# Second mixer: input chunks 5 to 7 go by token blocks behind the levels of the decayed scores

## The reference

```
cq, ckv, krope, gq, gk, gv, gg, lr_f, lr_b = _split(x @ w_in, ODD_SPLITS)
...
mla = _merge(_blocked_attention(q, k, v, (MLA_NOPE + MLA_ROPE) ** -0.5))
def log_gate(lr, w2, bias):
    return _heads(jax.nn.log_sigmoid((lr @ w2 + bias).astype(F32)) / GLA_TAU, GLA_HEADS)
gq_h = _heads(gq, GLA_HEADS) * (GLA_K_DIM ** -0.5)
o = _bidirectional_scan(gq_h, _heads(gk, GLA_HEADS), _heads(gv, GLA_HEADS), log_gate(lr_f, ...), log_gate(lr_b, ...))
gla = _merge(_rms_norm(o, gla_norm)) * jax.nn.silu(gg)
return jnp.concatenate([mla, gla], axis=-1) @ w_out
```

## Time and profile before

| | us |
|---|---|
| median of 3 runs | 2326.71 |
| lowest and highest | 2320.91, 2326.8 |
| span of the profiled execution | 2323.1 |
| TensorE busy in it | 2166.1 |
| VectorE busy | 1142.2 |
| ScalarE busy | 784.0 |

### The profile page before, as it was taken

How to read it: one execution, slowest core, us unless ns; L and a number is a source line. 1 busy time by engine, 2 the same in 40 slices (tenths; PEclk the granted TensorE clock), 3 DMA queues, 4 the chain that set the end, 5 groups by cost and what they waited for, 6 DMA issues and landing times.

```text
span 2323.1 us, 30109 instructions
## 1 busy us (share of the span) xinstructions
PE 2166.1 (93%) x12126; PEld 1528.0 (66%) x12126; DVE 1142.2 (49%) x1786; ACT 784.0 (34%) x1299; POOL 61.5 (3%) x62
## 2 busy tenths in 40 slices
PE   8999998899887989997988999999999999989998
PEld 7884443443367944433433688898888788888887
DVE  5582222121156831211111666678666766787666
ACT  3441110111034321101111355454555455554553
POOL 0010000000010100000000000001000000001000
PEclk9999999899998799999999999999999999999999
DMA  9449999999972289999999864634555464534561
GB/s 289 145 175 379 421 421 421 417 421 420 413 246 73 76 363 420 420 421 415 420 420 421 295 209 168 199 128 127 181 200 200 154 208 166 193 96 159 167 208 46
DMA packets 231542, 622.66 MB, mean 268 GB/s; under 512 B 15456, under 2 KB 166944, under 8 KB 182112
## 3 DMA queue, kind: packets, MB, share of 16 engines
q1 hardware_dynamic: 226096, 605.32, 68.7%
q0 software_dynamic: 3040, 10.78, 1.5%
q10 hardware_dynamic: 2256, 4.50, 0.5%
HBM read 619.51 MB, written 1.05 MB: 267 GB/s over the span
## 4 chain that ended last, share of the span: by engine, by line
PE 41%; DMA 6%; DVE 4%; ACT 2%; issue 1%; POOL 0%; SPq 0%; DVEq 0%; ACTq 0%
PE bank L1517 14%; PE bank L1505 10%; PE bank L1518 7%; PE bank L228 6%; PE bank L1345 3%; DMA arena<-in_moe_w_up 1%; DMA ring<-in_moe_w_up 1%; DMA ring<-in_ffn_gate 1%; DMA w_parts<-in_moe_w_up 1%; DMA x_tok<-in_moe_w_up 1%; DVE w_low L439 1%; PE bank L1673 1%; ACT w_high L432 1%; DVE x_tok L687 0%; DVE x_tok L676 0%
## 5 line engine op out<-in xcount | busy, mean ns | idle before, releaser
L439 DVE TENSOR_TENSOR w_low<-ring,w_high 128x1024 fp32r<-128x1024 f32 x364 | 441.1, 1225 | 271.7 <-ACT w_high L432 271.7
L1517 PE MATMUL bank<-xT_parts,w_high 128*128 128x512 f32 x1408 | 496.2, 395 | 6.0 <-DVE xT_parts L504 6.0
L432 ACT ACTIVATE w_high<-ring 128x1024 fp32r<-128x1024 f32 x364 | 377.1, 1053 | 218.0 <-PE bank L1518 184.6
L1518 PE MATMUL bank<-xT_parts,w_low 128*128 128x256 f32 x1408 | 394.5, 280 | 0.0
L1345 PE MATMUL bank<-ring,arena 128*64 128x512 f32 x1344 | 339.0, 594 | 17.3 <-DMA w_parts<-in_moe_w_gate 5.3
L1517 PEld LDWEIGHTS bank<-xT_parts,w_high 128*128 128x128 f32 x1408 | 264.0, 188 | 69.0 <-DVE xT_parts L504 6.9
L1345 PE MATMUL bank<-w_parts,arena 128*64 128x512 f32 x768 | 263.8, 609 | 13.4 <-DMA w_parts<-in_moe_w_up 6.7
L1518 PEld LDWEIGHTS bank<-xT_parts,w_low 128*128 128x128 f32 x1408 | 265.8, 189 | 3.1
L1345 PEld LDWEIGHTS bank<-ring,arena 128*64 128x64 f32 x1344 | 110.1, 137 | 230.5 <-issue 221.9
L1453 DVE SCALAR_TENSOR_TENSOR arena<-arena,bank 128x512 f32<-128x512 f32 x32 | 23.9, 747 | 434.1 <-PE bank L1345 434.1
L228 PE MATMUL bank<-w_high,xT_parts 128*128 128x256 f32 x1152 | 222.9, 290 | 10.4 <-DVE w_low L439 8.8
(11 more groups left out here) (284 smaller groups left out, 2934.4 us busy)
## 6 DMA issues: line engine op xcount, KB each, us to landing
ring<-in_moe_w_gate SPq DMA_DIRECT2D x56, 1024.0 KB, 24.3
ring<-in_moe_w_up SPq DMA_DIRECT2D x56, 1024.0 KB, 21.0
ring<-in_moe_w_down SPq DMA_DIRECT2D x56, 1024.0 KB, 25.8
ring<-in_ffn_gate SPq DMA_DIRECT2D x44, 1024.0 KB, 6.8
ring<-in_ffn_up SPq DMA_DIRECT2D x44, 1024.0 KB, 5.4
ring<-in_ffn_down SPq DMA_DIRECT2D x44, 1024.0 KB, 6.6
w_parts<-in_moe_w_up SPq DMA_DIRECT2D x32, 1024.0 KB, 26.1
w_parts<-in_moe_w_down SPq DMA_DIRECT2D x32, 1024.0 KB, 26.1
```

Source lines behind the costliest of these rows:

```text
L432: e.activation(hi, src, ACT.Copy).then_inc(*S.high.tell(key))
L439: e.tensor_tensor(lo, src, hi.bitcast(F32), ALU.subtract).then_inc(*S.low.tell(key))
L1517: e.matmul(pairs(bank[:, :]), hi[:, j, :], k.x_parts[:, :, j, :], start=j == 0, stop=False)
L1518: ins = e.matmul(bank[:, 0:T], lo[:, j, :], k.xh[:, j, :], start=False, stop=j == KT - 1)
```

## The change

Chunks 5, 6 and 7 leave the attention. The list loses its "project" entries. A table `OD_ROUNDS` says which token block of which chunk TensorE does behind which step of the levels: both blocks of 5 behind the diagonal and level 8, of 6 behind levels 7 and 6, of 7 behind levels 5 and 4. ScalarE copies each chunk out after its second block, and `OD_SPLITS` puts the split of chunk 7 behind that of level 8, and the split of output chunk 0 behind level 6; VectorE takes its part of those splits one step later. The split of chunk 6 moves ahead of the attention, behind the copy of chunk 4.

```diff
--- before.py
+++ after.py
@@ -1901,9 +1901,11 @@
 
 
 
-OD_ORDER = (("scores", 0), ("scores", 2), ("project", 5), ("gates", 0), ("probs", 0), ("probs", 2), ("project", 6), ("logs", 0),
+OD_ORDER = (("scores", 0), ("scores", 2), ("gates", 0), ("probs", 0), ("probs", 2), ("logs", 0),
             ("turn", 0), ("turn", 2), ("gates", 1), ("values", 0), ("values", 2), ("logs", 1),
             ("scores", 1), ("scores", 3), ("probs", 1), ("probs", 3), ("turn", 1), ("turn", 3), ("values", 1), ("values", 3), ("mix", 0), ("mix", 1))
+OD_ROUNDS = {0: (5, 0), 2: (5, 1), 3: (6, 0), 4: (6, 1), 5: (7, 0), 6: (7, 1)}
+OD_SPLITS = {2: ("od_in", 0, 7), 4: ("od_out", 0, 0)}
 ROPES = slice(MLA_NOPE, MLA_QD)
 
 
@@ -2004,9 +2006,7 @@
     project_pe(e, k, od(4))
     out_banks = [k.banks.open(e, O_BANKS, ("mla_o", pair)) for pair in range(2)]
     for what, i in OD_ORDER:
-        if what == "project":
-            project_pe(e, k, od(i))
-        elif what == "scores":
+        if what == "scores":
             view = pairs(k.banks.open(e, B_BANKS, ("mla", i))[:, :])
             e.wait_ge(*S.dve_step["q_roped", i // 2])
             e.wait_ge(*S.act_out["k_raw", 1])
@@ -2025,8 +2025,14 @@
             for j in range(2):
                 ins = mm(e, view[:, j, :], [(k.gla_w2[rank, block(j)], b.narrow_T[rank, 0, :])])
             ins.then_inc(*S.product.tell(("gate_log", i)))
-    project_pe(e, k, od(7))
-    decayed_pe(e, k, b.streams, lambda step: None)
+
+    def beside(step):
+        if step in OD_ROUNDS:
+            c, tb = OD_ROUNDS[step]
+            bank = k.banks.open(e, A_BANKS, od(c)) if tb == 0 else k.banks[od(c)]
+            project_block_pe(e, k, od(c), bank, tb)
+
+    decayed_pe(e, k, b.streams, beside)
     decayed_values_pe(e, k, ("gla_o",), b.streams, b.crosses, lambda side, i: 2 * i + side, b.gla_v, od(5))
     gated_pe(e, k, "od_out", 0, ("gla_o",), ("mla_mix",))
 
@@ -2055,10 +2061,9 @@
             e.wait_ge(*S.product[key, pair])
             evacuate_act(e, k, (key, pair), tile[r, 2 * pair:2 * pair + 2, :], pairs(k.banks[key, pair][r, :]))
     od_project_act(e, k, 4, b.gla_v[:, :, 0:256])
+    split_chunk(e, k, od(6), split_act)
     for what, i in OD_ORDER:
-        if what == "project":
-            od_project_act(e, k, i, b.gla_v[:, :, 256:512] if i == 5 else b.gate[:, :, 0:256])
-        elif what == "scores":
+        if what == "scores":
             if i % 2:
                 e.wait_ge(*S.product["mla_pt", i - 1])
             softmax_act(e, k, ("mla", i), b.e1[i // 2], MLA_QD ** -0.5, k.tags[:, i // 2, :])
@@ -2074,8 +2079,16 @@
                 e.wait_ge(*S.masks_made["all"])
             e.wait_ge(*S.product["mla_o", 2 * i + 1])
             evacuate_act(e, k, ("mla_o", i), k.mixT[:, 2 * i:2 * i + 2, :])
-    od_project_act(e, k, 7, b.gate[:, :, 256:512])
-    decayed_act(e, k, b.streams, lambda step: None)
+
+    def beside(step):
+        if OD_ROUNDS.get(step, (0, 0))[1]:
+            c = OD_ROUNDS[step][0]
+            projected(e, k, od(c))
+            evacuate_act(e, k, od(c), (b.gla_v if c < 6 else b.gate)[:, :, 256 * (c % 2):256 * (c % 2) + 256])
+        if step in OD_SPLITS:
+            split_chunk(e, k, OD_SPLITS[step], split_act)
+
+    decayed_act(e, k, b.streams, beside)
     e.wait_ge(*S.act_out[od(7)])
     e.activation(b.gate, b.gate, ACT.Silu).then_inc(*S.act_out.tell(("gla_o", "gate")))
     e.wait_ge(*S.act_out["mla_o", 1])
@@ -2139,11 +2152,10 @@
         e.wait_ge(*S.dve_step["q_cos", pair])
         e.tensor_tensor(part, part, tmp, ALU.add).then_inc(*S.dve_step.tell(("q_roped", pair)))
     split_chunk(e, k, following(k, od(4)), split_dve)
+    split_chunk(e, k, following(k, od(5)), split_dve)
     for what, i in OD_ORDER:
         tags = k.tags[:, (i // 2) % 2, :]
-        if what == "project":
-            split_chunk(e, k, following(k, od(i)), split_dve)
-        elif what == "scores":
+        if what == "scores":
             softmax_dve(e, k, ("mla", i), MLA_QD ** -0.5, tags)
         elif what == "probs":
             e.wait_ge(*S.act_out["mla", i])
@@ -2171,10 +2183,14 @@
     for i in (1, 3):
         e.wait_ge(*S.product["mla_o", i])
     e.memset(b.diag.rearrange("p a b c -> p (a b c)"), 0.0).then_inc(*S.dve_step.tell("gla_clear"))
-    split_chunk(e, k, following(k, od(7)), split_dve)
     e.wait_ge(*S.dve_step["la", 1])
     e.wait_ge(*S.act_out[od(3)])
-    decayed_dve(e, k, b.streams, lambda step: None)
+
+    def beside(step):
+        if step - 1 in OD_SPLITS:
+            split_chunk(e, k, OD_SPLITS[step - 1], split_dve)
+
+    decayed_dve(e, k, b.streams, beside)
     mix_parts_dve(e, k, k.mixT[:, 0:4, :], (slice(0, P), slice(0, 4), slice(0, T)), ("mla_mix",))
     gated_dve(e, k, "od_out", 0, ("gla_o",), k.gla_norm[:, :], b.gate, ("gla_o", "gate"), norm)
```

## The result

| | before | after |
|---|---|---|
| median | 2326.44 (5 runs, 2320.91 to 2326.8) | 2332.06 (5 runs, 2327.96 to 2334.08) |
| ratio | | 1.003, interval 1.0019 to 1.0041 |
| profiled span | 2323.1 | 2325.8 |

The medians are 5.6 us apart, the ratio says +7.0 us (4.4 to 9.5). Forecast were +9.8 and 2336, with 64% on slower. The spans differ by only 2.7 us, and that difference misleads. Columns as in the earlier trace rows.

What follows compares the result with a forecast made beforehand. TensorE, busy 93% of the span, was taken as the bound, with VectorE also packed in the levels. Levels +12.8, attention -7.3 and clock +4.3 gave +9.8 us on 2326.7, so 2336.5; range 2324 to 2345.

Steps and rivals of the forecast that it cites:

- Attention, -7.3: Before the levels' sums: chunks 5 and 6 leaving TensorE's row gives 4.7 us, memset and moved split 2.6; sums 7.3 sooner.
- No change up to level 8: From the sums' start to the widest level's second stream: 9.45 us as before, block (5, 0) costing nothing.
- Stall 3.2: Behind block (5, 1): TensorE idles 3.2 us while ScalarE copies the chunk, splits chunk 7, then copies the cross scores.
- The clock, +4.3: In the levels: slow TensorE clock adds 1.7 us each to blocks (5, 1) and (6, 0), 0.6 and 0.3 to level products.
- Level products at 1.7 a stream: In the levels: one stream of one level, 16 products, takes 1.7 us on TensorE at the fast clock.
- TensorE sets the pace: After the stall: level pair with block takes TensorE 6.3 us, VectorE needs 4.1 a level; second-narrowest level begins 12.8 later.
- The last three levels as before: End of the levels: the three levels without blocks run at VectorE's 4.1 us each, unchanged.
- The mixer's end goes through one for one: Behind the mixer: experts' weights stream once buffers are free, so any shift of its end reaches the total in full.
- Rival B: In the levels: the clock stays up through the blocks; +5.5 us, 2332; chance 20%.
- C: In the levels: the clock falls again between blocks, each of five costing 4.6 us; +16, 2343; chance 18%.
- E: In the attention: slow clock costs scores and turns, so it gains less; 3 us above the likeliest case, 2340; chance 6%.
- D: In the levels: TensorE isn't the pace, stall gone; -2.6 us, or -5.5 with clock up into the values; chance 14%.

Runs made afterwards that it cites:

- its own experiment: Kernel before with one edit: VectorE's split of output chunk 0 moved behind the passes that follow the last mask; 2320.64, ratio 0.9989.
- short blocks: Changed kernel with the six token blocks in the levels cut to 2 of 24 products each, copies, splits and waits kept; 2322.77, ratio 0.9995.
- one chunk early: Against the changed kernel: chunks 5 and 6 in attention waits, only chunk 7 in the levels, behind diagonal and level 8; 2318.76, ratio 0.9975.
- the last experiment: Against one chunk early: VectorE's split of output chunk 0 moved out of the levels, behind the passes after the last mask; 2314.54, ratio 0.9961.

## Why the prediction was right, step by step

The forecast, slower by 9.8, stands against 7.0 and 9.5 measured. The sum held in both halves, but not each term of it: in the levels two errors of 3.6 and 2.7 us lay in opposite directions, which is luck.

- **Attention, -7.3: measured -8.3.** The turns and gates ran at the slow clock as assumed (1.94 and 2.07). VectorE took the second gates 13.2 us behind the queries (711.04 less 697.86) instead of 18.3 (720.13 less 701.86), 5.1 sooner where 4.7 stood. Memset to sums went from 3.54 to 0.83, so the split gave 2.7, predicted 2.6; its own experiment, in the kernel before, gave 3.9 in the trace and 2.6 in the time.
- **No change up to level 8: right.** From the start of the sums to the end of level 8, 10.6 us after and 10.7 before. The block behind the diagonal was free.
- **Stall 3.2: measured 2.94,** with the releaser that was named. But it was priced alone. Taken away, it gave back 5.9 us, since level 7 and block (6, 0) behind it then ran fast as well.
- **The clock, +4.3: mis-sized, about 7.0.** Against the fast rows of the same trace: block (5, 1) 5.2 for 3.1 (1.7 predicted for the loss, 2.1 measured), level 7 4.6 for 2.6 (0.6 predicted, 2.0), block (6, 0) 5.4 for 3.1 (1.7, 2.3), level 8's second stream 1.24 for 0.72 (0.3, 0.5). I had let 4.0 us of slow rate suffice in block (6, 0), as in the earlier trace rows; here nearly the whole block was slow. And I knew no fast level, so I could not price a slow one.
- **Level products at 1.7 a stream: mis-sized, 1.3.** 32 products take 2.60. I took the row with 64x128 products as the nearest; those of 64x64 are quicker. Nine streams from level 7 on make this 3.6 us too much, which hides the 2.7 us missing in the clock; the rest is small, above all blocks of 3.1 us from start to start instead of 2.94 and a level pair of 3.12 (below).
- **TensorE sets the pace: right.** VectorE waits 4.73 us for TensorE at level 5 (757.36), and TensorE's row has no gap from level 7 to the last block. Its steps are 10.0 us with the slow block and then 5.6 to 6.1, where 6.3 stood, so the sign "levels 7 to 4 each over 6 us" did not come. From level 8's second stream to the second-narrowest level 38.4 us (736.29 to 774.66), where the sum had 38.4 (34.1 plus 4.3).
- **The last three levels as before: right.** From that row of VectorE to the last mask 11.6 us, 11.6 before.
- **The mixer's end goes through one for one: nearly.** Of the 8.7 and 8.5 us 6.6 and 6.7 reached the end in the same traces.

Rival B (clock up throughout) and C (down at every block) are out by the windows; E (attention gains less) has the wrong sign. D needed the stall gone and the clock up; with both, the time was -1.2 us against its -2.6, so its condition was well named. Its reason was not: TensorE was still busy without a gap (10.00 of 10 us), a pair with its block took 5.6 us and not 5.1, and the levels were 7.0 us longer than before where D had 4.7. Its 1.08 us a stream was nearer to the 1.3 than my 1.7.

The experiments showed one thing that the prediction did not have: of the +17.0 us, 9.1 went with the blocks' products (short blocks), and 8.0 stayed: 3.1 for the order on ScalarE, 2.2 for one split on VectorE, and 2.7 for TensorE's level pairs at the half clock. I had written that the two splits lie beside TensorE's longer row. That of chunk 7 costs nothing, in short blocks either, since it lies in the wait for ScalarE. That of the output chunk is hidden only because the row is so long: in the changed kernel it made TensorE's next pair 3.12 us long instead of 2.60, in short blocks it cost 2.2, and with one chunk early, where VectorE paces the levels, some 3, as the last experiment shows.

## What to carry to other kernels

A stretch in which TensorE looks half asleep may still have no room: ask which engine paces it, and what each moved piece brings for that engine, not only for the one with the gaps. Move the work into the longest real wait (here three blocks between the last values and level 8, which cost 0.3 us) and stop there; of the three chunks one could stay in the levels with a gain, two or three could not. A wait of 3 us on TensorE costs its length and the clock behind it, so price both. And set the traces to zero at the last unchanged instruction before spans are compared; here the spans differed by 2.7 us, and by 6.6 when counted from there, where the change cost 7.0 and 9.5.

## What the hardware showed that I had not expected

- Long stretches of level products stayed at the half clock: 48 us at 0.50 with TensorE busy for 38.3 (short blocks), 26 us at 0.50 with 24.1 busy (one chunk early). In the levels and behind them, what stood ahead of each return was a dense block or the 128x128 value products.
- The clock also fell without a long wait ahead of it: behind the last block of the changed kernel it was 1.00 for the 20 us up to 776, 19.72 of them busy, and 0.51 for the next 10, 9.40 busy, with level products alone; the longest idle there was 0.28 us. Why, no run here shows.
- A level product of 64x64 starts every 0.08 us at the fast clock and every 0.135 to 0.146 at the slow one (2.60 and 4.67 us for 32; 21.09 for 156 in the earlier trace rows).
- The same unchanged code up to the end of the queries took between 697.6 and 705.7 us in thirteen traces, without any difference in the instructions.
